# Index scores of even and odd heads multiplied in turns into two PSUM banks

## The reference

```
dots  = einsum('bqhd,bsd->bqhs', qi, k_idx)        # 8 index heads, 64 wide, one shared key
score = einsum('bqhs,bqh->bqs', relu(dots), wi)    # weighted sum over the heads
score = where(key_pos <= qpos, score, -inf)
_, sel = top_k(score, 64)
logits = einsum('bqhd,bqkhd->bhqk', q, k[sel]) * scale ...
```

## Time and profile before

| | us |
|---|---|
| median of 3 runs (lowest, highest) | 1888.8 (1888.28, 1891.65) |
| the profiled execution, its time | 1892.16 |
| its span, first to last instruction | 1890.4 |
| PE busy | 1852.3 |
| POOL busy | 1515.8 |
| ACT busy | 950.4 |
| DVE busy | 929.7 |

### The profile page before, as it was taken

How to read it: one execution, slowest core, us unless ns; L and a number is a source line. 1 busy time by engine, 2 the same in 40 slices (tenths; PEclk the granted TensorE clock), 3 DMA queues, 4 the chain that set the end, 5 groups by cost and what they waited for, 6 DMA issues and landing times.

```text
span 1890.4 us, 28387 instructions
## 1 busy us (share of the span) xinstructions
PE 1852.3 (98%) x9850; PEld 1531.6 (81%) x9850; DVE 929.7 (49%) x2285; ACT 950.4 (50%) x1549; POOL 1515.8 (80%) x1298
## 2 busy tenths in 40 slices
PE   8999999999999999999999999999999999999999
PEld 6878888877888887788887688887887887788877
DVE  6774441456342345444157644326847354446534
ACT  4564453354444446454335645444647544545743
POOL 7868999885799977799976789987686886777785
PEclk9999999999999999999999999999999999999999
DMA  8445665555766554466545456654663655556453
GB/s 294 129 156 171 188 213 194 181 170 143 197 190 212 189 178 155 142 188 212 194 143 160 144 174 190 212 195 154 190 177 114 181 189 167 153 165 180 132 169 112
DMA packets 217076, 330.62 MB, mean 175 GB/s; under 512 B 11964, under 2 KB 109800, under 8 KB 216936
## 3 DMA queue, kind: packets, MB, share of 16 engines
q1 hardware_dynamic: 209024, 323.21, 54.8%
q10 hardware_dynamic: 7912, 5.59, 1.0%
HBM read 325.35 MB, written 3.41 MB: 174 GB/s over the span
## 4 chain that ended last, share of the span: by engine, by line
PE 90%; DVE 5%; DMA 2%; issue 2%; ACT 1%; POOL 1%; SPq 0%; DVEq 0%; ACTq 0%
PE acc L1480 19%; PE acc L1481 18%; PE acc L1487 16%; PE acc L1449 14%; PE acc L1450 7%; PE tps L1415 3%; PE acc L1502 3%; PE acc L1483 2%; PE ops L1544 2%; PE tps L1520 2%; POOL w_lo L1224 1%; PE acc L1439 1%; PE acc L1441 1%; PE acc L1440 1%; DMA raw<-in_w_mem_kv 1%
## 5 line engine op out<-in xcount | busy, mean ns | idle before, releaser
L1224 POOL TENSOR_TENSOR w_lo<-raw,w_hi 128x512 fp32r<-128x512 f32 (+2 forms) x1210 | 1474.9, 1251 | 334.0 <-ACT w_hi L1252 332.9
L1252 ACT CAST w_hi<-raw 128x1024 fp32r<-128x1024 f32 (+4 forms) x608 | 613.2, 1012 | 724.9 <-PE acc L1487 400.1
L1480 PE MATMUL acc<-w_hi,xT 128*128 128x512 f32 (+3 forms) x1168 | 451.3, 390 | 5.3 <-ACT U L1285 2.1
L1481 PE MATMUL acc<-w_lo,xT 128*128 128x512 f32 (+3 forms) x1168 | 434.2, 375 | 0.0
L1449 PE MATMUL acc<-xT,w_hi 128*128 128x512 f32 x1152 | 402.1, 394 | 0.0
L1487 PE MATMUL acc<-w_hi,xT 128*128 128x512 f32 (+3 forms) x1104 | 322.2, 373 | 0.0
L1450 PE MATMUL acc<-xT,w_lo 128*128 128x256 f32 x1152 | 319.5, 277 | 0.0
L1480 PEld LDWEIGHTS acc<-w_hi,xT 128*128 128x128 f32 x1168 | 221.1, 189 | 56.1 <-issue 16.9
L1449 PEld LDWEIGHTS acc<-xT,w_hi 128*128 128x128 f32 x1152 | 216.1, 188 | 50.1
L1481 PEld LDWEIGHTS acc<-w_lo,xT 128*128 128x128 f32 x1168 | 221.7, 190 | 32.2
L1487 PEld LDWEIGHTS acc<-w_hi,xT 128*128 128x128 f32 x1104 | 202.1, 189 | 38.0 <-DVE xT L1757 1.5
(11 more groups left out here) (220 smaller groups left out, 2257.0 us busy)
## 6 DMA issues: line engine op xcount, KB each, us to landing
raw<-in_w_gate_up SPq DMA_DIRECT2D x176, 512.0 KB, 3.9
raw<-in_w_in SPq DMA_DIRECT2D x104, 512.0 KB, 4.0
raw<-in_w_down SPq DMA_DIRECT2D x88, 512.0 KB, 4.4
raw<-in_w_out SPq DMA_DIRECT2D x48, 512.0 KB, 3.5
raw<-in_w_in_a SPq DMA_DIRECT2D x32, 512.0 KB, 4.3
raw<-in_w_in_b SPq DMA_DIRECT2D x20, 512.0 KB, 4.3
raw<-in_w_mem_kv SPq DMA_DIRECT2D x16, 512.0 KB, 4.2
raw<-in_w_in_c SPq DMA_DIRECT2D x16, 512.0 KB, 4.4
```

What stands on the lines that cost most here:

```text
L1224: ins = nc.gpsimd.tensor_tensor(lo[:, i:i + n], both[:, i:i + n], hi[:, i:i + n].bitcast(F32), ALU.subtract)
L1252: nc.scalar.copy(ring(w_hi, u.u % SPLIT, u), ring(raw, u.u % RAW, u)).then_inc(S["hi_ready"], 1)
L1480: nc.tensor.matmul(o, hi[:, tok], wh, start=first_k, stop=False)
L1481: ins = nc.tensor.matmul(o, hi[:, tok], wl, start=False, stop=False)
```

## The change

The PE task of an even group now also computes the odd group that follows it, and asks for both banks of `ops` at once. Inside it the matmuls go head by head in turns: even head into the first bank, odd head into the second. Its planned cost is 950. Relu and additions stay as they were, one task for each group and bank; both relus now wait for the joint PE task, and the next pair can only begin when the additions of both groups have released their banks.

```
             for i, gr in enumerate(groups):
-                gr.qk = qk
-                gr.turn = p.task("PE", "index", gr, 900, "index_ready", [b.take for b in qk], prio=0,
-                                 room=("ops", [(0,), (1,)]))
+                gr.qk, gr.bank = qk, i % 2
+                if not gr.bank:
+                    gr.odd = groups[i + 1]
+                    gr.turn = p.task("PE", "index", gr, 950, "index_ready", [b.take for b in qk], prio=0,
+                                     room=("ops", [(0, 1)]))
+                else:
+                    gr.turn = groups[i - 1].turn
...
-                bank = ops[:, gr.turn.slot[0], :]
+                bank = ops[:, gr.turn.slot[gr.bank], :]
...
-                for i, h in enumerate(gr.heads):
-                    base = HD * (h % 2)
-                    ins = nc.tensor.matmul(ops[:, k.slot[0], w * i:w * i + w],
-                                           heads_of(gr.queries)[base:base + HD, h // 2, P * gr.t:P * gr.t + P],
-                                           heads_of(gr.keys)[base:base + HD, 0, 0:w], start=True, stop=True)
+                for i, pair in enumerate(zip(gr.heads, gr.odd.heads)):
+                    for half, h in enumerate(pair):
+                        base = HD * half
+                        ins = nc.tensor.matmul(ops[:, k.slot[half], w * i:w * i + w],
+                                               heads_of(gr.queries)[base:base + HD, h // 2, P * gr.t:P * gr.t + P],
+                                               heads_of(gr.keys)[base:base + HD, 0, 0:w], start=True, stop=True)
...
-                    relu, weight = ops[:, gr.turn.slot[0], w * i:w * i + w], wi[:, gr.t, h:h + 1]
+                    relu, weight = ops[:, gr.turn.slot[gr.bank], w * i:w * i + w], wi[:, gr.t, h:h + 1]
```

More of the change, by code:

```diff
@@ L252, in __init__ @@
         self.keys = keys
+        self.odd = None
+        self.bank = 0
         self.qk = []
```

## The result

The changed kernel takes 1895.57 us (median of 8 executions, 1890.09 to 1903.78), the kernel before 1890.03 us on the same chip (8, 1888.28 to 1892.42). The ratio is 1.0034, 95% interval 1.0023 to 1.0045: slower by 0.34%, where 1883.7 us and a gain were forecast. The profiled execution of the changed kernel is the shortest of its 8, 1890.09 us with a span of 1888.3 us. So there are two questions: why this one gained nothing, and what adds 5.5 us to the median.

What follows compares the result with a forecast made beforehand. PE was taken as the bound (busy 1852.3 of 1890.4 us, 90% of the chain). Gains of 2.9 us in block 0 and 2.2 in block 3, 5.1 together, took the median 1888.8 to 1883.7 us; range 1881.7 to 1888.8.

Steps and rivals of the forecast that it cites:

- the 3.95 us bound: Index pairs of tile 1: emptying both banks lets the next pair start about 3.95 us after one begins; PE needs 1.26.
- the 6.1 us of the sum: PE time saved by index pairs: 0.54 us for tile 0 plus 2.52 for tile 1, 3.06 a block, 6.1 in both.
- The rival that the streams do not overlap: Index matmuls into the two `ops` banks do not overlap, so nothing is gained: 1888.8 us, chance 0.05.
- The slower rival: PE stands before the second and third pair until additions free both banks: up to 10.8 us lost, 1893.5 at most; chance 0.10.
- the last addition: End of index additions before the top-k: 13 to 16 us after the first pair, so top-k starts within half a microsecond of before.
- the start of the third pair: Third index pair in a block: by the planner's numbers no earlier than 9.22 us after the first.
- the second rival: Attention's end: DVE and ACT no earlier at the mask, PE waits; gain only 1 to 3.5 us, 1885.3 to 1887.8; chance 0.27.
- as I had priced that rule: PSUM emptying as bound: if the skill's rule held for time too, the whole gain would be gone, 1888.8 us.
- the sign that I had named for this: Block 3's attention: forecast wrong if PE's idle time grew from 4.0 us by about what the pairs gave.
- a way to slower: Mask before masked attention: coming over 5 us later would also make the kernel slower; within the slower rival's chance of 0.10.

Runs made afterwards that it cites:

- the old order: Kernel before with its planned order untouched, but each even group's matmuls issued in turns at the odd group's place: 1888.62 us, ratio 0.9992 to the kernel before.
- the second look: The changed kernel without edit, profiled once more to catch a long execution, the later of two such single profiles: 1897.34 us.

## Why the prediction was wrong

**What holds.** What a pair costs: 1.09, 1.06 and 1.06 us, forecast 1.10, 1.06 and 1.06. A block has three idle stretches of the weight loads, of 0.33 to 0.36 us, in place of five (the one of 0.36 us stands in front of the first pair, before and after). The pairs lie 6.3 and 6.2 us apart, over the 3.95 us bound, and PE has no wait for `scores` in front of them. PE's busy time falls by 7.5 us in the first pair of profiles and by 4.6 in the second, on either side of the 6.1 us of the sum. (The sum would not have been quite the same by either way of counting, as I wrote: a full halving of the first pair's 1.64 us is 0.82 us, where the sum had 0.54; measured were 0.55.) The rival that the streams do not overlap is out. The slower rival's mechanism was not the changed kernel's: it showed only in the old order, at 2.5 and 1.3 us.

**The step that failed** is the last addition, "So the top-k starts about when it did, half a microsecond either way", and with it "So DVE can follow by some 3 us, but with little to spare". I had allowed 13 to 16 us from the first pair to the last addition, compared that with block 3's 15.4 us, and called it no change; in block 0 it had been 13.2. It became 16.9 us in both blocks, with 3.00 and 2.98 us of it an idle DVE. The term mis-sized is the start of the third pair: 9.22 us after the first was the earliest that the room allows, and I took it for about the time that the order would give. The pairs lie 6.3 and 6.2 us apart, so it started at 12.5 us.

The error is one of reading: I looked for idle time of PE in front of a pair, where the wait for two banks is covered by products, and not for what DVE, whose 31 us of work to the mask come after the last pair, can do in between. Its transposes also stood behind that pair. The top-k's first instruction comes 2.5 us later after the first pair than before in block 0 (78.15 - 59.97 against 75.21 - 59.56 us) and 1.5 us later in block 3, and the mask 2.9 us later in both. Of the 1.4 us added in between in block 3, 0.3 are the longer addition (1.26 us against 1.00); the rest I did not trace. PE's idle time in block 3's attention grew from 4.0 to 6.3 us, the sign that I had named for this.

That is the second rival (1885.3 to 1887.8), carried to its end: on the spans of the profiled executions the gain is nil, 1888.3 us for the changed kernel against 1890.4 and 1887.7 us for the two profiles of the kernel before, whose median of 1890.03 is as long as the changed kernel's shortest execution (1890.09). The Trainium skill says (TensorEngine Tiling (Array Packing), PSUM Bottleneck) that tiling does not speed up the emptying of PSUM, which may become the bottleneck. In the short executions the whole gain is gone, as I had priced that rule. But the trace does not show the speed of the emptying as the bound, as DVE stood idle for 3.00 us in the middle of it. What cost was the order that the planner made around the wait for two emptied banks: two more banks for the second pair are worth 4.3 us with the masks in the first addition in both kernels, and 10 us without.

**What the prediction did not have at all** is the other 5 us. It named a mask later by over 5 us as a way to slower, but no mechanism for it; in the long executions index to mask is 57.9 and 56.9 us, 8 and 7 more than before. The first instruction in front of the top-k has two operands in SBUF and meets an unbroken run of POOL's subtractions, in this order as in the one before. In this order it is held up by 2.5 us more in some executions, three of five profiles and by the times most, and PE's clock falls behind it. Taking the instruction away takes away 4.6 us and the long executions, which is the experiment that shows it; doubling it adds 4 to 5 us, of which up to 3 could be its own price; taking it away from the kernel before changes nothing. The Trainium skill has the rule (SBUF — State Buffer, Who interferes with whom): a VectorE instruction with two SBUF inputs and a GpSimd instruction that reads SBUF exclude each other for a whole instruction. The trace agrees: every one of the 24 additions of this kind in the profiles ends 0.41 or 0.42 us behind the end of a subtraction, and where POOL has the next subtraction ready it takes about 1.6 us in place of 1.28. It goes further in that the addition does not always get its turn at the first end: 20 had it there, and four, of 3.71 to 3.75 us, only at the third.

**What stays open.** Why an addition gets its turn at the first end of a subtraction or only at the third, no run tells. In the kernel before it meets the same kind of run, begins 0.96 and 0.72 us into a subtraction, and was short in both of its profiles. In the changed kernel's order it begins 0.44 to 0.48 us into one in nine of ten cases, and was short in six of these and long in three. So the place within the subtraction sets the short length (the rest of the subtraction plus 0.41 us) but does not by itself decide between short and long; it was not varied by itself. How often an execution is hit follows only from the times, 16 of 19 above 1894 us, and from 3 of the 5 profiles of this plan. The other 2.6 us in a long execution are put to the clock because they fall into the stretch at half of it, and because the second look has a shorter stretch and less of them; the clock was not varied alone either. What decides a fall of the clock is open too, since the same waits in block 3's attention stand before one in one profile and before none in another.

## What to carry to other kernels

Before a change that asks for two buffers at once, follow the engine that empties them to its last use, and not only the engine that fills them: ask when its last piece of work starts, and what else waits for the same task. A faster TensorE pays only as far as that time moves forward, and spare banks may be worth as much as the faster matmul (here 4.3 us between two kernels with pairs, where the pairs in the old order gave 1.5 us, just within the noise; the spare banks without pairs were not run). When VectorE's work moves in time, see what GpSimd does at the new place; here the addition of masks and scores cost nothing that could be told once one operand still lay in PSUM. And take several profiles when the median lies above the profiled execution: the cause may be in those that the first one missed.

## What the runs showed of the hardware

- Two groups of index passes on the two halves of the rows overlap fully without turns when each is four passes of 256 columns (4 + 4 in 1.07 us, one group of 4 in 1.06), and in part when each is eight of 128 columns (8 + 8 in 1.64 us, in turns 1.09).
- VectorE's addition of two SBUF operands, 128 x 384 in float32, took 0.73 to 1.62 us or 3.71 to 3.75 us beside GpSimd's back-to-back subtractions of about 1.3 us. In all 24 cases it ended 0.41 or 0.42 us behind the end of a subtraction: in 20 the first that came, in 4 the third. Begun at the same point of a subtraction (0.44 to 0.48 us into it) it did either.
- After waits of 3.8 us (three profiles), 5.3 and 2.9 us TensorE's granted clock was at half speed, 1.2 in place of 2.4 GHz, for some microseconds; after waits of 1.3 us at the same place, and one of 1.9 us, it was not. In block 3's attention it fell in one profile behind two waits of 1.26 and 1.36 us, and in another with waits of 1.26 and 1.30 us it did not.
